# Four transformer layers on one core: other starting places for the split weight buffers and the units in SBUF

## What is computed

```python
def sqrelu_mlp(h, w1, w2):
    return jnp.square(jax.nn.relu(h @ w1)) @ w2
...
    for i in range(DEPTH):
        need_ctx = i < DEPTH - 1
        m_lat = (silu_c @ ada_w[i] + ada_b[i]).reshape(B, N_MOD, 1, D)
        h_lat = modulate(rms_norm(x_lat, norm_g[i, 0]), m_lat[:, 0], m_lat[:, 1])
        ...
        x_lat = x_lat + m_lat[:, 2] * rms_norm(y_lat, norm_g[i, 1])
        h = modulate(rms_norm(x_lat, norm_g[i, 2]), m_lat[:, 3], m_lat[:, 4])
        x_lat = x_lat + m_lat[:, 5] * rms_norm(sqrelu_mlp(h, mlp_w1[i], mlp_w2[i]), norm_g[i, 3])
```

## The kernel before

| tensors | bytes behind HH's place |
|---|---|
| HH, HL, raw, wh0 to wh4, wl0 to wl4, Gh, accl, ident, ones | 0 |
| UH, UL of all four layers, c_bh, c_bl, CQH, CQL, CKH, CKL | 480 |
| g_oh, g_ol | 128 |

## Time and profile before

### The profile page before, as it was taken

One profiled execution on the slowest core, in us unless ns is written; L12 is line 12 of the kernel. 1 busy time (PEld: TensorE's weight loads), 2 busy tenths in 40 slices (PEclk: granted clock), 3 DMA queues, 4 the chain that ended last, 5 costly groups with the idle time before them and its releaser, 6 DMA issues.

```text
span 1984.7 us, 27475 instructions
## 1 busy us (share of the span) xinstructions
PE 1946.9 (98%) x10285; PEld 1618.9 (82%) x10285; DVE 1402.2 (71%) x2243; ACT 898.6 (45%) x1536; POOL 254.2 (13%) x332
## 2 busy tenths in 40 slices
PE   8999999999999999999999999999999999989998
PEld 4877788888888777888888888888888878878897
DVE  5898777888766645487997676667755467567665
ACT  3433355333333453575554224634233354656554
POOL 2101010211111200411101001001100021331000
PEclk9999999999999999999999999999999999999999
DMA  8434235655653541367875432645555245337763
GB/s 307 133 99 136 75 105 182 204 182 178 194 179 98 166 155 33 105 228 248 267 239 159 147 99 74 199 150 181 161 171 157 77 150 173 94 96 234 224 187 109
DMA packets 191827, 315.12 MB, mean 159 GB/s; under 512 B 14637, under 2 KB 114312, under 8 KB 191696
## 3 DMA queue, kind: packets, MB, share of 16 engines
q1 hardware_dynamic: 162512, 210.09, 33.2%
q0 software_dynamic: 29184, 103.29, 17.2%
HBM read 312.29 MB, written 1.05 MB: 158 GB/s over the span
## 4 chain that ended last, share of the span: by engine, by line
PE 90%; DVE 4%; issue 2%; ACT 1%; POOL 1%; DMA 0%; SPq 0%; POOLq 0%; DVEq 0%; ACTq 0%
PE bank L708 26%; PE bank L715 24%; PE bank L714 24%; PE bank L718 8%; PE bank L713 2%; PE bank L711 2%; PE bank L770 1%; PE bank L794 1%; DVE acc L2251 1%; DVE wl L2226 1%; DMA raw<-in_ada_w 0%; PE bank L1100 0%; POOL wl L3169 0%; ACT junk L1627 0%; DVE X L2370 0%
## 5 line engine op out<-in xcount | busy, mean ns | idle before, releaser
L1595 ACT ACTIVATE wh<-raw 128x1024 fp32r<-128x1024 f32 (+4 forms) x390 | 399.9, 1032 | 573.4 <-PE bank L715 502.9
L2226 DVE TENSOR_TENSOR wl<-raw,wh 128x1024 fp32r<-128x1024 f32 (+3 forms) x372 | 439.5, 1190 | 244.4 <-ACT wh L1595 243.8
L708 PE MATMUL bank<-HH,wh 128*128 128x256 f32 (+1 forms) x1552 | 513.0, 331 | 2.9 <-DVE HH L2353 2.0
L715 PE MATMUL bank<-HH,wl 128*128 128x512 f32 (+1 forms) x1232 | 415.1, 337 | 0.0
L714 PE MATMUL bank<-HL,wh 128*128 128x512 f32 (+1 forms) x1232 | 414.9, 337 | 0.0
L2251 DVE SCALAR_TENSOR_TENSOR acc<-ada,sc,acc 128x512 f32<-128x512 f32 x518 | 362.5, 747 | 2.3
L708 PEld LDWEIGHTS bank<-HH,wh 128*128 128x128 f32 x1552 | 294.3, 190 | 30.1 <-issue 3.9
L708 PE MATMUL bank<-wh,UH 128*128 128x512 f32 x768 | 304.9, 397 | 0.0
L714 PE MATMUL bank<-wl,UH 128*128 128x512 f32 x768 | 303.3, 395 | 0.0
L715 PE MATMUL bank<-wh,UL 128*128 128x512 f32 x768 | 303.2, 395 | 0.0
L714 PEld LDWEIGHTS bank<-HL,wh 128*128 128x128 f32 x1232 | 232.3, 189 | 26.0 <-issue 0.2
(11 more groups left out here) (354 smaller groups left out, 2624.6 us busy)
## 6 DMA issues: line engine op xcount, KB each, us to landing
raw<-in_mlp_w SPq DMA_DIRECT2D x256, 512.0 KB, 4.3
ada<-in_mod_w POOLq DMA_DIRECT2D x96, 512.0 KB, 4.8
ada<-in_ada_w POOLq DMA_DIRECT2D x80, 512.0 KB, 4.6
raw<-in_ml_w_qkvo SPq DMA_DIRECT2D x28, 512.0 KB, 3.9
raw<-in_conv_w_in SPq DMA_DIRECT2D x24, 512.0 KB, 4.5
raw<-in_ada_w SPq DMA_DIRECT2D x12, 512.0 KB, 6.0
raw<-in_mla_w_o SPq DMA_DIRECT2D x8, 512.0 KB, 3.9
raw<-in_gla_w_v SPq DMA_DIRECT2D x8, 512.0 KB, 3.8
```

The lines of the kernel that those rows point to most:

```text
L708: pe.matmul(o, sh, mh, start=start, stop=False, skip_group_check=True)
L715: return pe.matmul(o, sl, mh, start=False, stop=stop, skip_group_check=True)
L1595: act.activation(k.wh[n % NSPL][:, 0:m], k.raw[(NDIRECT + n) % NRAW][:, 0:m], ACT.Copy).then_inc(*k.w_hi.up("w hi", n))
L2226: dve.tensor_tensor(k.wl[n % NSPL][:, 0:m], k.raw[(NDIRECT + n) % NRAW][:, 0:m], k.wh[n % NSPL][:, 0:m].bitcast(F32), ALU.subtract).then_i ...
```

## The change

Only places in SBUF change. The five pairs become slices of one tensor `split`, pair i 0, 8, 16, 32 and 128 bytes behind HH's place (SPLIT_AT counts floats); high and low part of a pair share their offset. The units get a pad in front: UH and UL of layers 0 to 3 lie 0, 64, 256 and 192 bytes behind HH's place. Pads bring CQH, CQL, CKH, CKL, c_bh, c_bl, g_oh and g_ol to 0. To make room, three small tensors (st_cq, st_p, den) move into free columns of Y and `grow` (five rows of gains) into Pl0. What lies between the pairs and the shared area (ada, acc, gb, ident, ones, ta, tp and the small tensors) moves back by 128 bytes. The instructions of every engine and their order stay as they were: PE has the same 9006 rows in its program, and one of them reads its operand from Pl where it read grow.

```diff
@@ -21,6 +21,8 @@
 NSPL = 5
 NADA = 3
 NDIRECT = 12
+SPLIT_AT = [0, 2, 4, 8, 32]
+UNITS_AT = [0, 16, 64, 48]
 
 CONST_SLICES = {}
 
@@ -535,8 +537,9 @@
 
         self.Gh = sb("Gh", [128, 2, D], F32R)
         self.raw = [sb(f"raw{i}", [128, 1024]) for i in range(NRAW)]
-        self.wh = [sb(f"wh{i}", [128, 1024], F32R) for i in range(NSPL)]
-        self.wl = [sb(f"wl{i}", [128, 1024], F32R) for i in range(NSPL)]
+        split = sb("split", [128, 2 * NSPL * 1024 + SPLIT_AT[-1]], F32R)
+        self.wh, self.wl = [[split[:, (2 * i + j) * 1024 + SPLIT_AT[i]:(2 * i + j + 1) * 1024 + SPLIT_AT[i]] for i in range(NSPL)]
+                            for j in range(2)]
         self.ada = [sb(f"ada{i}", [128, 2, 512]) for i in range(NADA)]
         with ExitStack() as s1:
             self.acc = sb("acc", [128, 2, 2, 512], F32, s1)
@@ -561,27 +564,27 @@
...
 
         with ExitStack() as s1:
+            sb("cq_pad", [128, 104], F32, s1)
             self.CQH, self.CQL = sb("CQH", [128, 3, 512], F32R, s1), sb("CQL", [128, 3, 512], F32R, s1)
             self.CKH, self.CKL = sb("CKH", [128, 2, 512], F32R, s1), sb("CKL", [128, 2, 512], F32R, s1)
...
-            self.grow, self.gcol = sb("grow", [5, 128], F32, s1), sb("gcol", [128, 5], F32, s1)
+            self.gcol = sb("gcol", [128, 5], F32, s1)
...
             self.qr = [sb(f"qr{i}", [128, 512], F32, s1) for i in range(2)]
             self.Pl = [sb(f"Pl{i}", [128, 512], F32, s1) for i in range(4)]
             self.Pc = [sb(f"Pc{i}", [128, 256], F32, s1) for i in range(4)]
+            self.grow = self.Pl[0][0:5, 0:128]
             self.PTl, self.PTc = sb("PTl", [128, 4, 256], F32, s1), sb("PTc", [128, 2, 256], F32, s1)
-            self.st_cq = sb("st_cq", [128, 2, 4, 4], F32, s1)
-            self.st_p = sb("st_p", [128, 2, 4, 4], F32, s1)
+        self.st_cq, self.st_p = [self.Y[:, o:o + 32].rearrange("p (a b n) -> p a b n", a=2, b=4) for o in (4160, 4192)]
...
         self.U = []
         for li in range(4):
             with ExitStack() as s1:
-                if li == 2:
-                    pass
+                sb(f"u_pad{li}", [128, 104 + UNITS_AT[li]], F32, s1)
                 self.U.append((sb(f"UH{li}", [128, 8, 512], F32R, s1), sb(f"UL{li}", [128, 8, 512], F32R, s1)))
...
@@ -608,8 +611,10 @@
                 self.gqt = [self.gqt, qt]
                 self.AT = [sb(f"g_at{r}", [128, 4, 128], F32, s2) for r in range(2)]
             with ExitStack() as s2:
+                sb("g_o_pad", [128, 64], F32, s2)
                 self.gOH, self.gOL = sb("g_oh", [128, 8, 256], F32R, s2), sb("g_ol", [128, 8, 256], F32R, s2)
         with ExitStack() as s1:
+            sb("c_pad", [128, 104], F32, s1)
             self.BH, self.BL = sb("c_bh", [128, 8, 512], F32R, s1), sb("c_bl", [128, 8, 512], F32R, s1)
...
@@ -624,7 +629,7 @@
...
-            self.den = sb("m_den", [128, 8, 2, 2], F32, s1)
+            self.den = self.Y[:, 4192:4224].rearrange("p (h a t) -> p h a t", h=8, a=2)
             with ExitStack() as s2:
                 self.mKC, self.mKW = sb("m_kc", [128, 2, 512], F32, s2), sb("m_kw", [128, 2, 256], F32, s2)
                 self.VCe = sb("m_vc", [128, 2, 8, 129], F32, s2)
@@ -1544,7 +1549,7 @@
...
-        pe.transpose(b[:, 0:5], k.grow[:], k.ident[0:5, 0:5]).then_inc(*b.filled())
+        pe.transpose(b[:, 0:5], k.grow, k.ident[0:5, 0:5]).then_inc(*b.filled())
...
 
...
```

## The result

The changed kernel takes 1989.11 us, the median of 20 runs (1986.25 to 1991.21), against 1986.22 us for the kernel before (20 runs, 1981.68 to 1989.34). The ratio is 1.0016, 95% interval 1.0009 to 1.0023: 2.9 us slower. That is clear of noise and within the 0.3% that the prediction called no change, where it forecast 10 us slower.

The account below looks back on a forecast made before the run. It took PE's matmul pace to bound the kernel. Terms of 12.7 + 0.9 - 2.3 - 1.3 - 0.1 made 9.9 us more, forecast as 1996.5 us, with a range of 1977 to 2006.

Parts of the forecast that it names:

- What bounds the kernel: Whole kernel: PE busy 1946.9 of 1984.7 us, so time is about matmul count times pace; only the pace can change.
- 512 columns beside HH: Products of HH or HL with a pair: four blocks in five leave distance 0, 6.0 ns each, 12.7 us more.
- The units, c_bh and g_oh: Pairs over these: 2.3 us back at distance 0 or 256, 1.3 us from other distances, 0.1 us from g_oh.
- 320 and 384 columns: The 192 matmuls of these widths: four fifths pay 6.0 ns each, 0.9 us more.
- 256 columns: Narrow matmuls streaming HH or HL: 2227 leave distance 0 at no cost, 0; bounds -3.1 and +14.9 us.
- narrow matmuls pay too: Rival: all 2227 displaced matmuls of 256 columns pay 6.7 ns, 24.8 us more in sum, 2011 us; chance 0.12.
- small displacements count as none: Rival: pairs 8 and 16 bytes off behave like 0, only pairs 3 and 4 leave; 1985.5 us; chance 0.22.
- A better place than HH's own: Rival: some distance is cheaper than 0, found by pairs 1 and 2; -21 us, 1965 us; chance 0.20.
- the place does nothing: Rival: the pace step belongs to something else that comes with the units; time stays 1986.5 us; chance 0.06.

Follow-up runs that it names:

- third kernel: The changed kernel with all pairs, all units, c_bh, g_oh, CQH and CKH at HH's place; 1969.86 us, ratio 0.9917 to the kernel before.
- the second: The changed kernel with all pairs back at HH's place, so only units and the rest move; 1972.82 us, ratio 0.9936 to the kernel before.

## Why the prediction was wrong

*What bounds the kernel* held. The other engines' busy times changed by at most 2.5 us, all of them less, and the difference is in the distances of matmuls.

*512 columns beside HH* held. 6.0 ns for four of five blocks made 12.7 us; measured were 11.4. The range of 230.8 to 233.3 in the four displaced pairs is where g_oh and the 32 column product stood. 8 bytes cost 4 ns where HH is streamed, less than I took, but not 0, and 6 to 7 ns where the pair is.

*The units, c_bh and g_oh* held in size: -3.7 us forecast, -2.7 measured. Blocks that meet at 0 or 256 do not reach 226.7 as a whole (the mean of the units' blocks at distance 0 is 228.4). Blocks of other distances stand before them, and the low pace comes only some way in: the first six matmuls of these blocks have 229 to 234 ns on average, and those from the tenth on 226.4 to 227.2.

*320 and 384 columns* were put at +0.9 us by the price of 512. They have next to none in this kernel: 146.6 before and 146.8 ns after at 320. That is no rule, for with all pairs 8 bytes off the 320 columns have 148.0.

*256 columns* is the step that failed. I took 0 and had -3.1 us as the lower bound; measured were -4.4 us. The row I went by, a single matmul at a border, is one of eight whose mean is 118.5 ns, lower than the stretch in the earlier trace rows. I read that as the end of a range and not as what it was, the only matmul of this width beside an operand at a distance. The third kernel bears this out: with the units at HH's place the same eight have 120 ns each. The four displaced pairs' means over the trace are 115.9, 118.4, 118.3 and 118.8 ns at 8, 16, 32 and 128 bytes, 117.8 together, and 2227 x 2.0 = 4.5 us.

*Stalls* had no term. The short waits and starts between stretches came out 2.8 us shorter after, of which 2.0 lie where one trace has half the granted clock and the other the full one, and 2.3 shorter with the pairs alone. The third kernel and its repetition have spans of 1968.4 and 1972.1 us from one and the same program, although their paces agree: in the repetition PE waits 3.1 us for DVE at 1620.8 us, and has half the clock (0.50) from 1623.3 to 1626.7. So single traces differ by as much, and I don't put these down to the change.

So with the narrow term right the sum would have been 9.9 - 4.4 = 5.5 us. The sizes of the other terms (-1.3 beside HH, +1.0 at the units, c_bh and g_oh, -0.9 at 320 to 384 columns) bring it to 4.3, and the stalls' -2.8 to 1.5, which is the difference of the two spans. In 20 runs each the difference is 2.9 us with an interval of 1.8 to 4.6. The 4.3 without the stalls lies in that interval, so the paces account for the measured time. The direction was right, and nearly half of the price forecast was given back by matmuls that I had counted as untouched.

*The rivals.* That narrow matmuls pay too had the sign wrong. That small displacements count as none falls with 230.8 and 233.3 ns at 8 and 16 bytes; its time, 1985.5 us, was nearer than the forecast's by chance. A better place than HH's own exists at 256 columns and was not found at 512. That the place does nothing had the nearest time of all, 1986.5 us, by chance as well, since a cost of 11 us and gains of 7 nearly cancel; it falls with the second and third kernels. With it falls the sum of 0 that the prediction drew from the Trainium skill (TensorE: Matmul & The Clock Gate, "Step-by-step: what each phase is for"): where the two operands begin makes a matmul cost anything from 226.7 to 238.3 ns here. Whether it is the load and the stream that meet, or something else, no run shows. The chances were added up wrongly by 0.01: slower is 0.48, and within 0.32.

Ahead of the prediction I wrote that no stationary operand is used for two matmuls in a row. The high part is, in two of the three, in the order of lines 708, 714 and 715; it is loaded for each, as the equal counts of matmuls and loads in the earlier trace rows show.

## What to carry to other kernels

Where float32r matmuls of 512 columns run back to back with a load for each, put the moving and the stationary operand at the same place in a line of 256 bytes: it was 226.7 ns a matmul against 229 to 238 here, and 16 us of 1986. Do it for all the parts of a product, since one in three out of place costs as much as all. A width that shows no price at one distance is no neutral ground: cost it as unknown on both sides, and let the one odd matmul in the trace pull the value and not only the bound.

## What was not expected of the hardware

- At 256 columns equal places are not the best ones: 119.8 ns at distance 0, 115.6 with the pairs 8 bytes off and 115.1 at 64, but 120.0 with HH 8 bytes earlier. What decides there stays open; the order of the three parts matters too (113.4 and 117.8 ns at 64 bytes).
- 4 bytes off is worse than 8 or 12: 236.7 against 233.5 and 229.0 ns for a pair streamed over the units of layer 0.
- POOL's subtraction of the low parts got faster with the pairs 8 bytes off, 2095 for 2509 ns, with the same 18 blocks. Block by block it is about 400 ns less, 2.4 to 2.0 us, where the pair lies 4, 8 or 24 bytes behind `raw`, and no less at 12, 16, 32, 48, 64 or 128, nor with wl alone 8 bytes off, so it goes with the place of wh beside `raw`, both of which POOL reads, and not with that of its output. Why is not shown, and it lies beside the path. The rows of the third kernel and of the one with all pairs 8 off:

```profile
L3174 POOL TENSOR_TENSOR split<-raw,split 128x1024 fp32r<-128x1024 f32 x18 | 44.9, 2509 | 34.2 <-ACT split L1600 34.2
```

```profile
L3174 POOL TENSOR_TENSOR split<-raw,split 128x1024 fp32r<-128x1024 f32 x18 | 37.5, 2095 | 37.0 <-ACT split L1600 37.0
```
